# Other passes over the tokens: 128, 256, 256, 256 and 128, with the eight sample rows in the last

## The reference, cut to what matters

```python
xn = rmsnorm(x); z = xn @ w_in                       # 3360 columns, and three gates of 1024
ya = window attention(q, k, v)                       # window 128: a tile needs keys and values of the tile before
yb = trailing means of windows 2, 4, 8, 16
yc = mLSTM, chunks of 128, with a carried state C, n, m
x += (sigmoid(ga) * (ya @ w_a) + sigmoid(gb) * (yb @ w_b) + sigmoid(gc) * (yc @ w_c)) @ w_out
xb = rmsnorm(x); q = xb @ peer_wq                    # 8 heads, two halves of 128
v1, i1 = top_k(q1 @ k1.T, 16); v2, i2 = top_k(q2 @ k2.T, 16)
top_v, experts = top_k(v1 + v2 of all 256 pairs, 16); gates = softmax(top_v)
act = gelu(xb . u[experts]); x += sum over 128 experts of gates * act * v[experts]
```

## The kernel before

| pass | norm, project, branches | merge, output, norm, find |
|---|---|---|
| 0 | none | 48, all in find (`KEPT[0]`) |
| 1 | 80 | 144 |
| 2 | 112 | 144 |
| 3 | 112 | 144 |
| samples | 112, of them 24 at point `x` | 128 |

## Time and profile before

### The profile page before, as it was taken

The page is one execution under the profiler, slowest core; times in us unless marked ns, Lnnn a source line. Parts: engine busy times, 40 slices in busy tenths (PEclk is TensorE's granted clock), DMA queues, the critical chain, the costliest instruction groups (busy, mean ns, idle before and its releaser), DMA issues. The chain is left out here.

```text
span 4008.1 us, 37442 instructions
## 1 busy us (share of the span) xinstructions
PE 3339.7 (83%) x12654; PEld 2199.9 (55%) x12654; DVE 2295.9 (57%) x5276; ACT 1116.3 (28%) x3389; POOL 1270.5 (32%) x1148
## 2 busy tenths in 40 slices
PE   8698779879989798689989897789987886388797
PEld 8577547656666476356665574556654332255451
DVE  0411893574557677555657676745667675535444
ACT  1210342342223334332223333422134232121221
POOL 0100333433323333433323333424333343123331
PEclk9789989989999899789989898799999999676886
DMA  4134889779999898689999897889999999699895
GB/s 155 50 104 157 333 341 359 308 293 394 421 392 393 345 420 369 270 333 413 421 375 412 357 421 299 328 335 421 421 365 403 384 421 405 247 361 407 339 421 144
DMA packets 211432, 1356.19 MB, mean 338 GB/s; under 512 B 24249, under 2 KB 28393, under 8 KB 77456
## 3 DMA queue, kind: packets, MB, share of 16 engines
q0 software_dynamic: 148736, 1082.20, 67.2%
q1 hardware_dynamic: 59047, 259.01, 17.0%
q10 hardware_dynamic: 3456, 12.58, 0.8%
HBM read 1337.44 MB, written 17.53 MB: 338 GB/s over the span
## 5 line engine op out<-in xcount | busy, mean ns | idle before, releaser
L1784 POOL DMA_INDIRECT arena<-uv,eidx x1024 | 1173.5, 1146 | 2395.6 <-PE ps L795 1830.5
L795 PE MATMUL ps<-arena,dgs 128*128 128x512 f32 x3340 | 1640.6, 636 | 217.8 <-ACT dgs L1104 211.9
L1332 DVE CUSTOM_DVE_ANT_0 arena<-arena,xx 128x1024 f32<-128x1024 f32 x1024 | 1238.7, 1227 | 630.2 <-DMA arena<-uv,eidx 605.4
L795 PEld LDWEIGHTS ps<-arena,dgs 128*128 128x128 f32 x3340 | 653.2, 203 | 955.9 <-issue 667.8
L1088 ACT ACTIVATE gel<-dots 128x2 f32<-128x2 f32 x512 | 103.5, 202 | 1565.5 <-DVE dots L1332 1564.1
L828 PEld LDWEIGHTS ps<-wbuf,xT 128*128 128x128 f32 (+1 forms) x2304 | 389.4, 179 | 75.7 <-issue 53.6
L828 PE MATMUL ps<-wbuf,xT 128*128 128x210 f32 (+1 forms) x2304 | 428.8, 341 | 1.2 <-ACT xT L1122 1.1
L975 PE MATMUL ps<-xT,wbuf 128*128 128x256 f32 (+1 forms) x1920 | 411.3, 365 | 7.2 <-DMA wbuf<-w_merge 4.0
L975 PEld LDWEIGHTS ps<-xT,wbuf 128*128 128x128 f32 x1920 | 353.3, 201 | 86.5 <-issue 28.7
L1547 DVE SCALAR_TENSOR_TENSOR T<-T,ps 128x256 f32<-128x256 f32 (+1 forms) x120 | 44.3, 370 | 504.1 <-PE ps L979 488.9
L1104 ACT ACTIVATE dgs<-cst,wgt 128x128 f32<-128x128 f32 x835 | 300.0, 396 | 16.7
(11 more groups left out here) (348 smaller groups left out, 2144.0 us busy)
## 6 DMA issues: line engine op xcount, KB each, us to landing
wbuf<-w_merge SPq DMA_DIRECT2D x120, 768.0 KB
wbuf<-w_z SPq DMA_DIRECT2D x80, 840.0 KB
wbuf<-w_q SPq DMA_DIRECT2D x80, 512.0 KB
wbuf<-w_o SPq DMA_DIRECT2D x40, 512.0 KB
arena<-uv,eidx POOLq DMA_INDIRECT x1040
grow<-gains SPq DMA_DIRECT2D x10, 512.0 KB
xin<-x_prompt SPq DMA_DIRECT2D x4, 1024.0 KB
xs_scr<-R SPq DMA_DIRECT2D x4, 1024.0 KB, 3.9
```

What stands on the lines that cost most here:

```text
L795: done = mm(ps[:, half, :], dgs[:, j, :], ring[:, j, D + half * 512:D + (half + 1) * 512], start=(q == 0), stop=(q == P - 1), skip_group_c ...
L1332: v.tensor_tensor_reduce(ring[:, j, 0:D], ring[:, j, 0:D], xcur, 1.0, 0.0, ALU.mult, ALU.add, dots[:, j:j + 1]).then_inc(s["dotted"], 1)
L1784: g.indirect_dma_start(ring[:, j, :], None, uv, bass.IndirectOffsetOnAxis(ap=eidx2[:, tile_ // NT % 2, tile_ % NT, q:q + 1], axis=0)).then ...
```

## The change

There are five passes over the prompt, of 1, 2, 2, 2 and 1 tiles. The sample rows are the second tile, of 8 rows, of the last pass; their separate pass is gone. All five passes still load all weights. `merge` and the queries move 128 columns in pass 0, 256 in passes 1 to 3, and 136 in the last. The slots are given out anew:

| pass | norm, project, branches | samples | merge, output, norm | find | after it |
|---|---|---|---|---|---|
| 0 (tile 0) | none | | none | 32 | |
| 1 (tiles 1, 2) | 2 + 22 + 14 | | 48 + 8 + 2 | 48 | |
| 2 (3, 4) | 4 + 44 + 32 | | 74 + 12 + 4 | 54 | |
| 3 (5, 6) | 4 + 62 + 46 | | 74 + 12 + 4 | 54 | |
| 4 (7, samples) | 4 + 84 + 24 | 30 | 80 + 14 + 4 | 48 | 80 |

In passes 0, 1 and 4 all 8 heads are searched in `find`. The sample stage now has 11 points with 30 slots, and stands behind `branches` of tile 7; its loads on SyncE wait for the end of `branches` (`ycT_done`), and stand between the second and the third load of merge weights. The samples' search and its 16 gathers follow on the last tile's: the search runs among the last 80 slots (points `e`), the additions after the last slot. The small states move to other buffers.

```diff
-PASSES = 4
-TOK = SEQ // PASSES
-NT = TOK // P
+TILES = SEQ // P
+NT = 2
+TOK = NT * P
+PASSES = TILES // NT + 1
+LAST = PASSES - 1
...
+def prompts(p):
+    return range(1, 2) if p == 0 else range(1) if p == LAST else range(NT)
+def tiles_before(p):
+    return max(NT * p - 1, 0)
 def share_out():
-    first = [(("f", h, i), w if h else 0) for h in range(PH) for i, w in enumerate(FIND)]
-    find = [(("f", h, i), 52 / 16) for h in range(PH) for i in range(2)]
...
-    branch = [(("b", t, i), w * 44 / 48) for t in range(NT) for i, w in enumerate(BRANCH)]
-    late = merge + output + [(("n", 1), 4)] + find
-    stretches = [(0, first, KEPT[0])]
-    for p in range(1, PASSES):
-        project = [(("z", c, t), 60 / 32) for c in range(NZ) for t in range(NT)]
-        stretches += [(p, [(("n", 0), 4)] + project + branch, NT * P * p - P), (p, late, NT * P * p + KEPT[p])]
-    stretches += [(PASSES, [(("n", 0), 4)] + [(("z", c, 0), 84 / 16) for c in range(NZ)] + [(("x", 0), 24)], SLOTS - P),
-                  (PASSES, late, SLOTS)]
+    def chunks(p, projected):
+        return [(("z", c, t), projected / 32) for c in range(NZ) for t in range(NT)]
+    def branch(p, weight):
+        return [(("b", t, i), w * weight / 24) for t in prompts(p) for i, w in enumerate(BRANCH)]
+    def own_search(weight):
+        return [(("f", h, i), w * weight / 49 if h else 0) for h in range(PH) for i, w in enumerate(FIND)]
+    search = [(("f", h, i), 52 / 16) for h in range(PH) for i in range(2)]
...
+    sample = [(("x", i), 2.5) for i in range(SAMPLE_POINTS)]
+    tail = [(("e", i), 5) for i in range(16)]
+    stretches = [
+        (0, own_search(1), KEPT[0]),
+        (1, start + chunks(1, 32) + branch(1, 10) + merge + output + end, P), (1, own_search(1), P + KEPT[1]),
+        (2, start + chunks(2, 44) + branch(2, 16), 2 * P), (2, merge + output + end + search, 3 * P + KEPT[2]),
+        (3, start + chunks(3, 62) + branch(3, 23), 4 * P), (3, merge + output + end + search, 5 * P + KEPT[3]),
+        (4, start + chunks(4, 84) + branch(4, 24), 6 * P), (4, sample + merge + output + end, 7 * P),
+        (4, own_search(48) + tail, 8 * P)]
...
-KEPT = (48, 16, 16, 16)
-SOON = 4
+KEPT = (32, 48, 16, 16)
+SOON = (8, 8, 4, 4, 8)
+SAMPLE_POINTS = 11
...
-        zs = arena[0:NS, 0:ZW]
+        zs = arena[0:NS, ZW:2 * ZW]
...
+        def tiles_of(p):
+            return [(t, P) for t in prompts(p)] + ([(1, NS)] if p == LAST else [])
+        def columns(p):
+            return slice(P if p == 0 else 0, P + NS if p == LAST else NT * P)
...
+            sp.wait_ge(s["ycT_done"], TILES)
             sp.dma_start(k_s[:, 0:W - 1, :], cache_k[:, 1:W, :]).then_inc(s["kscr"], 16)
...
             load_c(0)
+            sp.wait_ge(s["kept"], 16 * 3)
+            sp.wait_ge(s["v_shift"], TILES + 1)
             load_c(1)
-            sp.wait_ge(s["evac_a"], NT * NZ * PASSES + 4 + NZ)
             sp.dma_start(scr_qk, zs[:, CQ0:CQ0 + 1024].rearrange("n (k m) -> n k m", k=2)).then_inc(s["c_scr"], 16)
...
-        def sample_vector(dve):
+        def sample_vector(dve, point):
...
-            dve.wait_ge(s["evac_a"], NT * NZ * PASSES + 4 + NZ)
-            sq = yT[0:NS, 0:3, :].rearrange("p a n -> p (a n)")[:, 0:640]
+            dve.wait_ge(s["ycT_done"], TILES)
+            point(LAST, "x", 0)
+            sq = T[0:NS, 0:640]
...
                 v.tensor_tensor(Cs, Cs, kb, ALU.add).then_inc(s["smp_v"], SMP["v"].step(f"c_cn{r}"))
+                point(LAST, "x", 6 + r)
...
-            topk(m, ssb, srep, 64, 1, e, eidx2[0:64, 0, 0:1, 0:PK])
+            topk(m, ssb, srep, 64, 1, e, eidx2[0:64, 1, 0:1, 0:PK], lambda i: point(LAST, "e", i))
...
-            for p in range(PASSES + 1):
-                tiles = tokens(p)[1]
-                weights(w_z, (KC, ZC), NZ, s["z_mm"], NT * NZ * p, tiles)
+            for p in range(PASSES):
+                tiles = len(tiles_of(p))
+                weights(w_z, (KC, ZC), NZ, s["z_mm"], NZ * tiles_before(p), tiles)
...
+                weights(w_merge, (12, P), 3 * KC, s["br_mm"], 3 * KC * p, 1,
+                        [store_states, lambda: sample_loads(sp, at)] if p == LAST else [],
+                        (s["pooled_ready"], NT * p + len(prompts(p)) + (0 if p else 1)))
...
                     for c in range(KC):
-                        last = mm(ps[:, 2 + 2 * b, 0:tok], wv[:, c, :], xT[:, c, 0:tok], start=(c == 0), stop=(c == KC - 1))
+                        last = mm(ps[:, 2 + 2 * b, m], wv[:, c, :], xT[:, c, m], start=(c == 0), stop=(c == KC - 1))
...
             for p in range(PASSES):
                 norm(p, 0)
                 project(p)
                 branches(p)
+                if p == LAST:
+                    sample_vector(dve, point)
                 merge(p)
                 output(p)
                 norm(p, 1)
                 find(p)
-            p = PASSES
-            norm(p, 0)
-            project(p)
-            point(p, "x", 0)
-            end_tile(TILES - 2)
-            sample_vector(dve)
-            merge(p)
-            output(p)
-            norm(p, 1)
-            find(p)
+            sample_experts_vector(dve, topk, point)
             end_tile(TILES - 1)
-            sample_experts_vector(dve, topk)
+            sample_add_vector(dve)
```

More of the change, by code:

```diff
@@ L459, in sample_scalar @@
             f(Ls, Ls, ACT.Exp, bias=anm, accum_out=ars).then_inc(s["smp_a"], SMP["a"].step("a_p"))
+            for i in range(6, 10):
+                point(LAST, "x", i)
             act.wait_ge(s["smp_v"], SMP["v"].at("c_hinv"))
@@ L615, in sample_experts_tensor, with sample_add_tensor @@
             for q in range(2):
-                last = mm(ps[0:64, 4 + q, :], sel, xs[0:NS, 0, q * 512:(q + 1) * 512], start=True, stop=True)
+                last = mm(ps[0:64, 6 + q, :], sel, xs[0:NS, 1, q * 512:(q + 1) * 512], start=True, stop=True)
             last.then_inc(s["smp_p"], SMP["p"].step("xb_mm"))
+            for i in range(16):
+                point(LAST, "e", i)
+        def sample_add_tensor(pe):
+            mm = nc.tensor.matmul
+            pe.wait_ge(s["s_evac"], 2 * PH * PASSES + 2)
             for j in range(PK):
@@ L805, in norm @@
             def norm(p, which):
-                rows_, tiles = tokens(p)
-                for t in range(tiles):
-                    n = norms(p, which, t)
-                    pe.wait_ge(s["xs_ready"], n + 1)
+                for i, (t, rows_) in enumerate(tiles_of(p)):
+                    pe.wait_ge(s["xs_ready"], norms(p, which, i + 1))
                     for c in range(KC):
@@ L833, in branches @@
             def branches(p):
-                pe.wait_ge(s["evac_a"], NT * NZ * (p + 1) + 4)
+                pe.wait_ge(s["evac_a"], NZ * tiles_before(p + 1) + 4)
                 pe.wait_ge(s["lf_ready"], p + 1)
                 pe.wait_ge(s["ones_set"], p + 1)
-                for t in range(NT):
-                    here, before = p * NT + 2 + t, p * NT + 1 + t
+                for t in prompts(p):
+                    here, before = NT * p + t + 1, NT * p + t
                     pe.wait_ge(s["qks_ready"], here)
@@ L1211, in merge @@
             def merge(p):
-                rows_, tiles = tokens(p)
-                tok = rows_ * tiles
+                m = columns(p)
                 for k in range(3 * KC):
@@ L1270, in _ @@
                 find(p)
-            p = PASSES
-            norm(p, 0)
-            project(p)
-            point(p, "x", 0)
-            sample_scalar(act)
-            merge(p)
-            output(p)
-            norm(p, 1)
-            find(p)
+            sample_experts_scalar(act, point)
             store_tile(TILES - 1)
-            sample_experts_scalar(act)
+            sample_add_scalar(act)
         @block.vector
@@ L1352, in norm @@
                     dve.wait_ge(s["scr_out"], 32 * p)
-                for t in range(tiles):
+                for t, rows_ in tiles:
                     v.scalar_tensor_tensor(xs[0:rows_, t, :], xin[0:rows_, t, :], rstd[0:rows_, t:t + 1], grow[0:rows_, :],
```

539 lines of the change are left out of this document (280 added, 259 removed).

## The result

The changed kernel took 4064.77 us (median of 4 runs, 4058.38 to 4070.24) beside 4005.61 us for the kernel before on the same chip (4003.71 to 4013.78): ratio 1.0143, 95% interval 1.0122 to 1.0164. The forecast was 3966 us. Its sum of 3967 us of span stands against 4061.0 us in the profile.

What follows compares the result with a forecast made beforehand. Transfers alone need 3221 of 4008 us; the other 787 are idle transfers, mainly first pass, branches and end. Passes of 398 + 703 + 780 + 863 + 1223 make 3967 us of span, forecast 3966; 8-in-10 range 3915 to 4038.

Steps and rivals of the forecast that it cites:

- Merge: (221.5 - 127.2) / 72 = 1.31 us a slot of TensorE; 127.2 + 48 x 1.31 = 190: Pass 1's merge: TensorE sets its length, 1.31 us for each of 48 slots, 190 us, above 165 us of transfers.
- Transfers at 0.7 of their rate in pass 1's merge: Sign to look for in pass 1's merge if the forecast holds: transfers at 0.7 of their rate.
- Sum 125: Last pass's sample stage: chain, 30 slots, late loads and slots that can't hide, 125 us; bounds 100 and 170.
- rival 2: Sample stage becomes the bound: at 170 us instead of 125 the total is 4011; decides from about 158; chance 0.16.
- 12: Sample stage of the last pass: 12 us for VectorE's slots that can't hide in the waits.
- TensorE as its limit: Old kernel's first pass, up to 398.3 us before any slot: DMA share 0.12 to 0.62 at most, TensorE the limit.
- 502 us more ahead of it: Whole kernel: one full pass of 863 us traded for 502 us more ahead of it and 322 in the last pass.
- 1, the last pass at the transfers' rate: Last pass: sample stage 100, merge 244, find 148; 50 us less, total 3916 us; chance 0.15.
- 3: Slower by TensorE's clock: pass 0 at 1.2 GHz, total 4030, or last 80 slots 274 us, total 4038; chance 0.17.
- By that rule pass 0 would run at half clock: Pass 0: by the skill's rule on short product bursts with DMA waits between, half clock; forecast took about 0.9.
- 4, 4006 us: Nothing is gained: errors of pass 1 and branches, about 10 to 15 us each, add up to 41; chance 0.09.

Runs made afterwards that it cites:

- the gate point: Changed kernel with all of pass 1's merge slots ahead of the gate product, between gate and branch products, instead of behind it: 4011.76 us.
- the early stores: Changed kernel with the last pass's cache and pooling-history copies and three z-row stores issued right after projection, not behind tile 7's branches: 4057.17 us.
- the order of the loads: On top of the gate point and the early stores, last rows stored before the states' loads, caches read before q and k loads: 3994.53 us.

## Why the prediction was wrong

**The step that failed first** is "Merge: (221.5 - 127.2) / 72 = 1.31 us a slot of TensorE; 127.2 + 48 x 1.31 = 190". As busy time it is right to 0.1 us, in part by luck: without the waits the same work keeps TensorE busy for 181.3 us. It fails as length: it put TensorE's waits at nothing. Its row has 72 slots in 24 chunks, pairs at both kinds of points, and TensorE waited only 10.7 us for diagonals. The plan put 48 slots all at the point with the shortest cover. The counts of the plan were read, the places were not. Price: 42.6 us, and 50.5 when taken away. The sign "Transfers at 0.7 of their rate in pass 1's merge" came true by luck: 289 of 421 GB/s are 0.69, but the forecast's own sum, 165 us of transfers in 190, asks for 0.87.

**The step that failed second** is the sample stage's "Sum 125", whose mechanism was right and whose size was rival 2's: 167 us, over the 158 that it named as the point where the gain is gone. The forecast charged "12" for slots that can't hide in waits. Measured, 30 slots cost 53 us and late loads 19, on a chain of 86 where 70 was known. The stores it called one wait, `c_scr`, held SyncE for 27 us from their issue, not 6 or 15.7, and they stood ahead of two more on the same queue.

**What held, and what only evened out.** Passes 2 and 3: 779.5 and 871.1 for 780 and 863. In pass 0 project 61.9 for 62, merge 92.5 for 87; find 139.5 for 131; first dot at 299.0 for 291. Setup was 16.4 for 21 and the branches 69.2 for 62, at a clock of 0.57; "TensorE as its limit" holds for project and merge of the old first pass, but in its branches TensorE was busy for 61.4 of 109.1 us. In pass 1 norm and project 131.4 for 133, find 206.9 for 202; its branches took 104.4, not 118. In the last pass norm and project 248.4 for 250, branches 105.8 for 104, the last 80 slots 199.0 for 202; but output and norm took 66.7, not 62, and find 168.8, not 160. Its merge was 238.6, not 257: with the transfers as limit it ran at all of their rate, and not at the 0.95 taken from the old one. The end was 69.9 us for 63: it is nearly all additions, 54.3 us as before, but with more ahead of the first of them than the 8 us that the forecast had:

```profile
L680 PE MATMUL ps<-arena,dgs 64*8 64x512 f32 x64 | 54.3, 1048 | 4.2 <-DVE dgs L736 4.2
```

The errors that go the other way, 14 us in pass 1's branches and 18 in the last merge, hide as much of the rest. ("502 us more ahead of it" should be 500.5, 398 + 703 - 600.5; the total does not use it.)

**The rivals.** 1, the last pass at the transfers' rate, held for merge alone. 2 came true in full, and would by its own sum have given 4011; the other 54 us no rival had. 3 is refuted at both ends: pass 0's project and merge had clocks of 1.00 and 0.95, the last 80 slots 0.99. The forecast also read the Trainium skill wrongly. "TensorE: Matmul & The Clock Gate", section "HAM oscillation", tells of products that take less time than the waits for DMA between them. In pass 0's project it was the other way round, with products for 3.1 to 7.8 us and waits of at most 1.7 us between; TensorE was busy for 50.6 of 61.9 us and the granted clock was 1.00. So "By that rule pass 0 would run at half clock" does not follow from that page of the Trainium skill, and this trace does not test it. 4, 4006 us, was 59 short of what the change took. With pass 1's merge mended the kernel takes 4011.76, near that figure, but by another way than small errors that add up. It is still 0.26% behind the kernel before, so with the sample stage as it is the new order of passes gains nothing.

**The change with its losses mended**: the gate point gives 53 us, the early stores 6, the order of the loads 11, and 12 more slots in the stage 9, to 3985.11 us, 0.52% ahead of the kernel before. The steps were measured on several chips, on which the kernel before took 4001.41 to 4005.61 us; by the ratios they are 47, 4, 14 and 14 us. 19 us are missing to the forecast's 3966. In the profile of this version, 23 us over the forecast's span, the passes take 411.9, 682.0, 786.6, 870.1 and 1239.8 us: 14 over in pass 0, 14 in passes 2 and 3, 17 in the last, and 21 under in pass 1. Whether the kernel before would gain as much from work of this kind was not tried.

## What to carry to other kernels

Work that passes over several engines in each loop turn needs its place read, not only its count: ask for each point what TensorE has between the start of that work and its use, and compare with the work's latency (here 3.6 us of cover for 6, 2 us lost a chunk). A range that is hit does not show its mechanism: the run with half of the pairs moved came out where it should, by waits of another kind. A stage that is a chain of loads is priced by its queue, issue by issue, with the landing times of the stage it moves into. Filling such a stage with other work paid here up to a DMA share of 0.94, and then turned sharply; take three counts before settling on one.

## What the runs showed of the hardware

Two stores of 33 KB together held SyncE's wait for 27 us, with 2.6 MB of copies and loads issued ahead of them on their queue since 3152 us and six gathers of 1 MB beside them; a 512 KB load took 15.7 in the earlier trace rows. That it is the queue ahead of a small transfer that counts fits the run with the early stores, where SyncE waited 17.5 us for two 4 KB stores behind 3 MB of loads, and with the loads moved behind them, 4.9 us; the share of the gathers in it was not taken apart. In the run without slots in the stage six gathers of later slots were issued just ahead of the two stores too, and the wait was 24 us.
